# Down products by seven half products: weight sums made by accumulating DMAs, in place of GpSimd differences and a scratch in DRAM

## The reference, cut to what matters

```
def conv_gated_ffn(h, w_up, conv_w, conv_b, w_down):
    u = h @ w_up                              # 1024 -> 2 * 2816
    ...                                       # depthwise convolution of width 3 over the tokens
    gate, val = jnp.split(u, 2, axis=-1)
    return (jax.nn.silu(gate) * val) @ w_down # 2816 -> 1024
```

## Time and profile before

| what | value |
|---|---|
| median of 3 runs | 1772.55 us (1769.37 to 1773.07) |
| span of the profiled execution | 1768.3 us, first to last instruction |
| PE busy | 1700.9 us, 96% of the span |
| DVE, ACT, POOL busy | 1045.2, 814.6, 448.2 us |
| DMA | 212.70 MB, mean 120 GB/s |

### The profile page before, as it was taken

One profiled execution on the slowest core, in us unless ns is written; L12 is line 12 of the kernel. 1 busy time (PEld: TensorE's weight loads), 2 busy tenths in 40 slices (PEclk: granted clock), 3 DMA queues, 4 the chain that ended last, 5 costly groups with the idle time before them and its releaser, 6 DMA issues.

```text
span 1768.3 us, 29693 instructions
## 1 busy us (share of the span) xinstructions
PE 1700.9 (96%) x12781; PEld 1393.5 (79%) x12781; DVE 1045.2 (59%) x1312; ACT 814.6 (46%) x1233; POOL 448.2 (25%) x403
## 2 busy tenths in 40 slices
PE   7998899999999999999999999999999999999999
PEld 6877787778887787888877887668888888788877
DVE  5477666545343565675677445874534356675667
ACT  5243555535553334443445235874554243453343
POOL 2001222120010373225410211450010066114620
PEclk9999999989999999999999999999999999999999
DMA  7210000133331475356533222003421375356623
GB/s 251 84 48 1 4 4 28 51 132 131 103 112 48 163 242 198 134 200 217 185 133 115 95 96 72 1 1 119 143 80 63 96 250 198 135 192 237 207 98 141
DMA packets 116925, 212.70 MB, mean 120 GB/s; under 512 B 4247, under 2 KB 50938, under 8 KB 116794
## 3 DMA queue, kind: packets, MB, share of 16 engines
q1 hardware_dynamic: 103239, 159.59, 26.8%
q0 software_dynamic: 13264, 51.09, 8.0%
q10 hardware_dynamic: 291, 0.12, 0.0%
HBM read 185.62 MB, written 25.17 MB: 119 GB/s over the span
## 4 chain that ended last, share of the span: by engine, by line
PE 71%; DVE 11%; ACT 7%; POOL 5%; issue 3%; DMA 3%; DVEq 0%; POOLq 0%; ACTq 0%
PE PS L440 46%; PE PS L547 10%; POOL DW L680 3%; DMA diff_dn<-DW 2%; DVE WLO L406 1%; ACT WHI L395 1%; PE PS L1908 1%; DVE SS L2211 1%; PE PS L1877 1%; PE PS L1220 1%; PE PS L946 1%; PE PS L1371 1%; PE PS L1333 1%; DVE AT L2223 1%; PE PS L2042 1%
## 5 line engine op out<-in xcount | busy, mean ns | idle before, releaser
L406 DVE TENSOR_TENSOR WLO<-WRAW,WHI 128x2048 fp32r<-128x2048 f32 (+1 forms) x106 | 248.7, 2357 | 296.5 <-ACT WHI L395 296.5
L440 PE MATMUL PS<-HIS,WHI 128*128 128x512 f32 x856 | 335.0, 391 | 4.2 <-DVE LOS L2386 1.5
L440 PE MATMUL PS<-HIS,WLO 128*128 128x512 f32 x856 | 333.2, 389 | 0.0
L440 PE MATMUL PS<-LOS,WHI 128*128 128x512 f32 x856 | 333.1, 389 | 0.0
L395 ACT ACTIVATE WHI<-WRAW 128x2048 fp32r<-128x2048 f32 (+1 forms) x107 | 203.1, 1907 | 230.5 <-PE PS L440 182.8
L440 PE MATMUL PS<-WHI,HIS 128*128 128x512 f32 x608 | 241.3, 397 | 1.1 <-DVE LOS L737 1.1
L440 PE MATMUL PS<-WLO,HIS 128*128 128x512 f32 x608 | 238.4, 392 | 0.0
L440 PE MATMUL PS<-WHI,LOS 128*128 128x512 f32 x608 | 238.0, 391 | 0.0
L440 PEld LDWEIGHTS PS<-HIS,WHI 128*128 128x128 f32 x856 | 160.7, 188 | 41.6 <-issue 3.2
L440 PEld LDWEIGHTS PS<-HIS,WLO 128*128 128x128 f32 x856 | 160.7, 188 | 33.6
L440 PEld LDWEIGHTS PS<-LOS,WHI 128*128 128x128 f32 x856 | 160.7, 188 | 33.1 <-issue 0.2
(11 more groups left out here) (326 smaller groups left out, 2845.5 us busy)
## 6 DMA issues: line engine op xcount, KB each, us to landing
WRAW<-ffn_w_up SPq DMA_DIRECT2D x88, 512.0 KB, 5.0
RW<-ffn_w_down POOLq DMA_DIRECT2D x22, 1024.0 KB, 7.3
diff_dn<-DW POOLq DMA_DIRECT2D x22, 1024.0 KB, 5.3
WRAW<-cross_wkv SPq DMA_DIRECT2D x16, 1024.0 KB, 5.0
PW<-diff_dn SPq DMA_DIRECT2D x8, 1536.0 KB, 8.9
WRAW<-diff_w_in SPq DMA_DIRECT2D x12, 1024.0 KB, 5.2
WRAW<-ab_w_in SPq DMA_DIRECT2D x10, 1024.0 KB, 5.6
PW<-diff_dn SPq DMA_DIRECT2D x8, 1280.0 KB, 7.6
```

Source lines behind the costliest of these rows:

```text
L406: V.e.tensor_tensor(part(WLO[place(i)], i), part(WRAW[raw_slot[i]], i), part(WHI[place(i)], i).bitcast(F32), ALU.subtract).then_inc(S("w_l ...
L440: mm = e.matmul(o, l, r, start=(si == 0 and kk == 0 and q == 0), stop=(si == len(steps) - 1 and kk == nk - 1 and q == 2))
```

## The change

The scratch in DRAM, the buffers `RW2` and `DW`, and POOL's subtractions (22 pairs of tiles in the program) are gone. Each combined weight is now a pure sum of quarters, made in the buffer `PW` itself: a first quarter is loaded, and each further one is loaded by a DMA that adds to what lies there (`accum_op=ALU.add`). Such DMAs are all issued from POOL. `SEVEN_SUM` lists the quarters (r, c) of each product. Product 6 starts from what product 1 left in its buffer (`SEVEN_ON`), so it needs two additions and no plain load. Signs that the sums no longer carry are put into POOL's sums of features and into the last step of products 2 and 4, which now subtracts.

```
-    PW_PLACE = (0, 1, 2, 3, 0, 1, 3)
+    PW_PLACE = (0, 1, 2, 3, 0, 3, 1)
...
+    SEVEN_SUM = (((0, 0),), ((0, 0), (0, 1)), ((0, 0), (0, 1), (1, 1)), ((1, 1),), ((1, 1), (0, 1)), ((1, 0),),
+                 ((1, 1), (1, 0)))
+    SEVEN_ON = 6
+    SEVEN_SP = (2, 3, 4, 5)
...
+    def load_weights(e, name, q, i=0):
+
         w, k0, n, _ = seven[name]
...
+        r, c = SEVEN_SUM[q][i]
+        if i:
+            e.wait_ge(*weights_in(name, q, i))
+        add = i > 0 or q == SEVEN_ON
+        src = w[k0 * P:(k0 + 2 * n) * P, c * 512:c * 512 + 512].rearrange("(p r q) n -> r q p n", r=2, q=P)[r]
+        to = PW[PW_PLACE[q]][:, 0:n, :]
+        dma = e.dma_start(to, src, accum_op=ALU.add) if add else e.dma_start(to, src)
+        dma.then_inc(weights_in(name, q, i + 1)[0], 16)
...
     def seven_pool(G, up, name):
...
-            G.e.wait_ge(S("w_lo"), seven[f"dn{l}0"][3] + 12)
-        for m in range(2):
-            load_pair(G.e, name, m)
+            G.e.wait_ge(S("w_lo"), seven[f"dn{l}0"][3] + 10)
+        load_weights(G.e, name, 0)
+        if name[3] == "1":
+            G.e.wait_ge(S("w_lo"), seven[f"dn{l}0"][3] + 14)
+        load_weights(G.e, name, 1)
         for gi in range(n):
-            for m in pairs_at(n, gi):
-                seven_weights_pool(G, name, m)
+            if gi == n - 1:
+                load_weights(G.e, name, 2, 1)
+                load_weights(G.e, name, 2, 2)
             seven_sums_pool(G, up, gi)
+            if gi == 0:
+                load_weights(G.e, name, 1, 1)
+        load_weights(G.e, name, 4, 1)
+        G.e.wait_ge(S("w_lo"), i0 + 4)
+        load_weights(G.e, name, 6)
+        load_weights(G.e, name, 6, 1)
...
-                        e.wait_ge(S("w_lo"), i0 + {2: 0, 4: 2, 5: 4, 6: 8}[q])
+                        e.wait_ge(S("w_lo"), i0 + {2: 0, 4: 2, 5: 8}[q])
```

More of the change, by code:

```diff
@@ L242, in build @@
     raw_level, raw_slot = [], []
-    seven, seven_piece, diff = {}, {}, {}
+    seven, seven_piece = {}, {}
     slot_total = [0, 0]
@@ L300, in seven_gemm @@
         shares(name, "g", done=14, ev=8)
-        shares(name, "seven", wdif=4 * n, shi=5, slo=5)
-        diff[name] = nc.dram_tensor(f"diff_{name}", (4, n, P, 512), F32, kind="Internal").ap()
+        shares(name, "seven", shi=5, slo=5)
         for i in range(seven[name][3], len(plan)):
@@ L370, in load_slab, with weights_in @@
             off += n
-    def load_weights(e, name, q):
+    def load_weights(e, name, q, i=0):
         w, k0, n, _ = seven[name]
[L375 to L384, removed]
+        r, c = SEVEN_SUM[q][i]
[6 more added lines that the diff above has]
+        dma.then_inc(weights_in(name, q, i + 1)[0], 16)
+    def weights_in(name, q, parts=None):
+        parts = len(SEVEN_SUM[q]) if parts is None else parts
+        on_sp = q in SEVEN_SP and parts == 1
+        each = [(x, i) for x in range(7) for i in range(len(SEVEN_SUM[x]))
+                if PW_PLACE[x] == PW_PLACE[q] and (x in SEVEN_SP and i == 0) == on_sp]
+        n = list(seven).index(name) * len(each) + each.index((q, parts - 1)) + 1
+        return S(f"seven_{'in' if on_sp else 'add'}{PW_PLACE[q]}"), 16 * n
     def hi_part(A):
@@ L526, in seven_pe @@
         w, k0, n, i0 = seven[name]
-        for q, (_, part_of, bank, fresh, _, _) in enumerate(SEVEN):
+        for q, (part_of, bank, fresh, _, _) in enumerate(SEVEN):
             if q >= 2:
@@ L556, in seven_operand_act @@
         A.e.wait_ge(*at(name, "done", 2 * q))
-        A.e.activation(SHI[SEVEN[q + 1][1]][:, 0:n, :], GX[:, SEVEN_RAW[q + 1], 0:n, :], ACT.Copy)\
+        A.e.activation(SHI[SEVEN[q + 1][0]][:, 0:n, :], GX[:, SEVEN_RAW[q + 1], 0:n, :], ACT.Copy)\
             .then_inc(sem(name, "shi"), 1)
     def seven_operand_dve(V, name, q):
-        n, x = seven[name][2], SEVEN[q + 1][1]
+        n, x = seven[name][2], SEVEN[q + 1][0]
         V.e.wait_ge(*at(name, "shi", q))
@@ L572, in seven_sum_dve @@
         x = X[:, 2 * t:2 * t + 2, c * 512:c * 512 + 512]
-        V.e.tensor_tensor(x, x, PS[:, bank:bank + 2, :], ALU.add).then_inc(sem(name, "ev"), 1)
+        V.e.tensor_tensor(x, x, PS[:, bank:bank + 2, :], ALU.subtract if q in (2, 4) else ALU.add)\
+            .then_inc(sem(name, "ev"), 1)
     def seven_last_sum_dve(V, name, t):
@@ L637, in seven_sums_pool @@
         e.wait_ge(*at(up, "sdif", 4 * gi + 3))
[L638 to L684, removed]
+        e.tensor_tensor(x(0), x(1), x(4), ALU.add).then_inc(sem(up, "sdif"), 1)
+    mem_level, dist_level = (16, 32), 16
     def seven_pool(G, up, name):
-        n, l = seven[name][2], name[2]
+        n, i0, l = seven[name][2], seven[name][3], name[2]
         if name[3] == "0":
@@ L1986, in evac @@
             elif (h, b) == (1, 0):
-                A.e.wait_ge(S("w_lo"), seven[f"dn{l}0"][3] + 14)
+                A.e.wait_ge(S("w_lo"), seven[f"dn{l}0"][3] + 12)
             A.e.activation(dst[:, :], PS[:, b, :], ACT.Identity, scale=convw(l, 1, cc),
@@ L2762, in _ @@
             last = {raw_slot[0]: 0, raw_slot[0] ^ 1: None}
-            first_weights = {seven[f"dn{l}{h}"][3] - 1: f"dn{l}{h}" for l in range(2) for h in range(2)}
             for i in range(1, len(plan)):
@@ L2791, in _ @@
                     load_x(e)
[L2792 to L2796, removed]
             for t, c, done in ((0, 1, 4), (1, 1, 5), (0, 0, 6), (1, 0, 7)):
```

12 lines of the change are left out of this document (5 added, 7 removed).

## The result

The changed kernel takes 1813.11 us (median of 4 runs, 1811.05 to 1816.36), the kernel before 1770.96 us beside it: a ratio of 1.0238 (95% interval 1.0222 to 1.0254), 42 us slower. The forecast was 1800 (28 us slower), with 1810 as the upper end of the likeliest case alone. The profiled execution's span went from 1768.3 to 1809.2 us, 40.9 more.

A forecast was written before the change was run, and what follows sets the result against it. PE bounds the kernel, busy 96% of the span. New waits for product 6's weights of 9 + 9 + 7 + 4 = 29 us, less 1.1, give +28: 1768.3 becomes 1796, with 4.3 to the median rounded to 1800; range 1769 to 1850.

The forecast's parts named there:

- my own case: Down products: additions priced at two moves make product 6's weights late; 1800 us, alone 1778 to 1810; chance 0.43.
- the case of three moves: Rival, down products: an addition fetches quarter, fetches sum and stores in turn, 14.6 us per 1536 KB; some 1860 us; chance 0.19.
- The chain's 5% of POOL: Rival, up products: removal gives more than PE's idle time; POOL's chain share would be tens of us; 1768 at best; chance 0.08.
- The term of 1.1 us: Up products: PE's idle time behind POOL, about 0.5 us in part 0, goes with the removal; 1.1 us for two layers.
- two moves: Price of an addition in the down products: two blocks fetched for one stored, 10.6 us for 1536 KB, 9.3 for 1280 KB.
- rivals of one move: Rival, down products: additions are as cheap as plain loads and nothing is late; 1771.5 us; chance 0.30.
- One us late at most: Product 2 in the down product: its second addition lands about 745 us, against a deadline of about 744.
- E: Time when the last features come, ahead of a down product: 736.22 us in the first; in the changed kernel's trace 731.64.
- (1): Sign: ACT's split waits for a DMA into `PW` ahead of product 6 in all four down products, with a PE gap.
- (2): Sign: landing time of an adding DMA of 1536 KB alone, 10.6 us; above 12 the three-move case is on.
- (3): Sign: the DMA share is near full from 740 to 785 us.
- (4): Sign: in the up products ACT's wait for POOL falls from 7.4 to 3.3 us everywhere, and PE's 0.5 us goes.

The follow-up runs named there:

- experiment 4: The changed kernel without the two additions to product 2's weights, so its output differs: 1798.21 us, ratio 1.0172 to the kernel before.
- experiment 3: The changed kernel without the two additions to product 6's weights, which takes what product 1 left without waiting: 1776.32 us, ratio 1.0038 to the kernel before.
- experiment 6: The changed kernel with product 2's first addition issued one group of features earlier on POOL: 1801.11 us, ratio 1.0182 to the kernel before.
- 7: The kernel of experiment 6 with product 4's quarter also loaded ahead of product 3's in SP's queue: 1775.73 us, on another occasion 1773.49 us.
- experiment 2: The changed kernel with every adding DMA made a plain load, same queues, waits and order, so its output differs: 1766.51 us, ratio 0.9987 to the kernel before.
- experiment 5: The changed kernel with SP's weight slabs for the next big product held until product 6's additions landed: 1801.05 us, ratio 1.0177 to the kernel before.

## Why the prediction was right, and where it was off

- **The time.** 1813 lies above the 1778 to 1810 of my own case. It is inside the stated 1769 to 1850 because that range reached up towards the case of three moves, which the runs rule out. The mechanism was right, its size was not.
- **What bounds the kernel, and the small gain: right in kind, too small.** The chain's 5% of POOL was no gain of tens of us; 3.2 us was all. The term of 1.1 us was mis-sized because I read idle time from PE's busy time alone. Matmul records overlap, so short gaps don't show there; the count of matmuls did (436 in 100 us of the earlier trace rows against 443). So the sentence that only 0.5 us comes through of POOL's lateness was wrong too: it was 1.6 us per layer.
- **The price of an addition: right.** I took two moves, 10.6 and 9.3 us; measured alone 11.3 and 9.9 (6 to 7% dearer), and 2.05 times the engines' time per MB. The rivals of one move and of three are out. That the destination has to be fetched too, as the Trainium skill has it ("DMA: Bandwidth & Descriptors", Rules for kernel authors), would give just this factor by my estimate of two moves; the runs show the factor, not the fetch. The fit on that page of the Trainium skill (Anatomy of one DMA), by which my estimate would have been 9.2 us, was short: the row was the better guide.
- **Product 2: right at PE, wrong in what hangs on it.** "One us late at most": PE waited 0.22 us in the first down product. Yet these additions were worth 11.7 us (experiment 4), since product 4's quarter shares the engines with the second one and the chain to product 6 starts behind it.
- **Product 6: right as what sets the end.** Its additions are 35 of the 42 us (experiment 3), and its weights' lateness is 43.5 of 46.9 us in the trace. I had not foreseen that products 4 and 5 come late too (ACT waited 8 to 9 us for each); it changes the picture, but not the sum: where product 6 is late, PE waits for it anyway. It would have counted with product 6 in time, as experiment 3 shows (6.7 us left over before).
- **The step that was off: the size of product 6's lateness.** Forecast 9, 7, 9 and 4, together 29 us; the rows give 13.3, 8.4, 11.7 and 10.1, together 43.5. In the first down product the chain starts at E + 16.1 where I had E + 14 (my "about 750" less 736.2), and from there it takes 38 us where I had 29.2 and about 7 for sharing. In part 1 of layer 1, where I took 4 us, it starts at E + 12.5 where I had E + 10, its two queued additions take 20.2 us where I had 16.0, and the last 11.4 where I had 9.3. I had read "nothing follows" as little sharing, but product 5's load alone sat beside the pair, and the additions were dearer than my price even where they ran alone (11.3 where I had 10.6, 9.9 where I had 9.3). With 43.5 + 3.4 (the rest of the length, 1.6 of it the clock in the third, which I had at nothing) less 3.0, the sum would have been 44 us, for the 42 measured.
- **The forecast signs.** (1) came as told ahead of product 6 in all four, and ahead of three more than I had named; (2) 11.3 for 10.6; (3) the DMA share was near full but for 744 to 752 us, where it was 0.37 and 0.53: the loads had landed and the next additions had hardly begun to move data; (4) in the up products ACT's wait for POOL is at most 3.6 us, as told.

## What to carry to other kernels

When single transfers become a chain in which each waits for the one before, write for each the time by which it is due and add up the chain from its first free start. At the given price of a link, the loss was decided here by *where the chain starts* and by what shares the engines with it. The step from experiment 6 to 7, in which the start moved from E + 12.0 to E + 4.9 in the first of four down products, gave back 27 to 30 us. What mattered was the last link's lateness, not the waits seen on the way or the slow matmuls that filled them. Full DMA engines make plain loads late that have nothing to do with the change: list what else is in flight until the last link lands. Small gains are read by counting matmuls in a fixed stretch, since busy time hides short gaps.

## What the runs showed of the hardware

- An adding DMA took 2.05 times the DMA engines' time of a plain one per MB (5.6 against 2.72 us, experiment 2); alone it landed after 11.3 us for 1536 KB and 9.9 for 1280 KB. The medians of the plain loads from the same queue were 7.0 and 6.4.
- A plain load of 1536 KB from SP issued while two additions were in flight landed after 18.2 us, with no slabs beside it (experiment 5), against 6.2 alone (698.63 in the changed kernel).
- An adding DMA also costs POOL more to issue: 1.43 to 1.46 us for 1536 KB, against 0.83 to 0.88 us for the plain load of the same shape in experiment 2.
- The packets of the queue rose from 13072 to 21520 for the same 51.09 MB. One addition of 1536 KB alone had 784 packets and took 8.8 us of the engines' time; SP's plain load of as many packets took 4.2, POOL's with 400 took 4.3.
- In the changed kernel the granted clock fell to 0.58 and 0.56 behind the second of two gaps (at 764.84 and 777.32), and was back at 1.00 in the window from 784; in the kernel before, with gaps of 1.0 us in its first down product and up to 2.4 in its second, it stayed at 1.00. In experiment 3 one gap was enough: behind the 3.89 us at 764.75 it was 0.73 from 764 to 768 and 0.85 in the next 4 us. In the changed kernel the drop cost the end nothing where product 6's weights were later still.
